# First weights' split moved ahead of the turned tiles in the opening of a hybrid encoder step

## Chip, cores and metric

One core of one Trainium2 chip runs the whole step in one launch. The metric is the device time in microseconds of that launch; the figures below are the median of three runs of the kernel before, its spread, and one profiled execution.

## The reference, cut to what matters

One layer of a streaming encoder is computed for a prompt of 512 frames and for 64 frames of a running stream, D = 1024. The opening is the first two lines of this:

```python
xn = rmsnorm(x, attn_pre_norm)     # x * rsqrt(mean(x*x) + eps) * gain
h = xn @ w_in                      # 1024 columns to keys, values, queries, gates, ...
# gated linear attention, indexed sparse attention, merge
x = x + rmsnorm(mixed, attn_post_norm)
f, conv_new = conv_ffn(rmsnorm(x, ffn_pre_norm), conv_prev, w_up, conv_w, conv_b, w_down)
x = x + rmsnorm(f, ffn_post_norm)
```

## The kernel before, in words

The program is written engine by engine, each engine's instructions in a fixed order, tied together by semaphores that each stand in the code. SP issues most transfers, ScalarE (ACT), VectorE (DVE) and GpSimd (POOL) compute, TensorE (PE) multiplies.

The 576 tokens stand in five tiles: tile 0 holds the 64 sample tokens, tiles 1 to 4 the prompt. TensorE multiplies rounded values (fp32r). To keep fp32 accuracy each operand is held as a rounded part and a remainder: `whi` and `wlo` for weights, `xhi` and `xlo` (both in the tile `xs`) for the turned samples. A product is then three matmuls. The weights come in panels through two buffers of `raw`; a panel's split is a copy with rounding on ACT (`split(p)`, line 960) and a subtraction on DVE (line 1531).

In the opening each tile tt takes these steps. SP loads it (`load_x`, line 607). ACT squares and sums it (`square`, line 975) and takes the root (`root`, line 980). DVE takes the reciprocal and scales the tile by it and by the gain, in two halves (`head`, lines 1542 and 1547); the gain row was spread over all partitions by PE into banks 3 and 4 (line 2124). PE turns the tile with eight transposes, two halves of four (`turn`, line 2111). ACT copies each half out with rounding (`turned`, line 987), and DVE takes the remainder (`rest`, line 1557).

The turned halves go through three PSUM banks in rotation: half t = 2 * tt + kh is in bank 5 + t % 3. So half 3, the second half of tile 1, uses the bank of half 0, and PE waits ahead of it for DVE's remainder of half 0:

```python
pe.wait_ge(xn_ready, t + 1)
if t >= 3:
    pe.wait_ge(xlo_ready, t - 2)
```

PE's order is: gain row, turn(0), turn(1), two products of the identity with itself into a bank that is overwritten afterwards (line 2145), eight products of the first weights' rounded part with tiles 0 and 1 (line 2134), the remainder products of tile 0 (lines 2139 and 2141), turn(2), those of tile 1, turn(3), then the other tiles with the first panel (lines 2087 to 2089), turn(4) among them, and the second panel. The first panel ("kv", 0) comes in four pieces, SP's first four `raw` transfers (line 620).

SP issues in this order: the gain row, tiles 0 and 1, the first panel, tiles 2 to 4, the second panel, the caches. Then it waits until all ten halves have their remainder (`xlo_ready` at 10) before it goes on with the small weight at line 663 and with panel after panel, each of which waits for the split two panels back.

Behind the opening come the other input panels with index scores, attention and the linear recurrence between them, the merge, and the ConvFFN with its products of w_up and w_down.

Of the kernel before, what the change touches and what calls it, by code (L numbers as in the profile page):

```python
# [18 lines left out]
P = 128  # L19
# [32 lines left out]
def tok(tt):  # L52

    return slice(0, P) if tt == 0 else slice(DEC + P * (tt - 1), DEC + P * tt)
# [7 lines left out]
def rows(tt):  # L62
    return DEC if tt == 0 else P
# [212 lines left out]
def splits(p):  # L276

    return p + 1 if p < DOWN0 else p + 1 - SEVENS
# [22 lines left out]
def layer_kernel(nc, A, O):  # L301
# [6 lines left out]
    with ExitStack() as ctx:  # L308
        base = (nc.sbuf_base + 63) // 64 * 64

        def at(name, shape, dtype, offset):
            size = 4
            for d in shape[1:]:
                size *= d
            assert base + offset + size <= nc.sbuf_usable_end, name
            return nc.alloc_sbuf_tensor_at(name, shape, dtype, offset=base + offset)

        def sem(name):
            return ctx.enter_context(nc.semaphore(name))

        ps = ctx.enter_context(nc.psum_tensor("ps", [P, 8, 512], F32))
# [9 lines left out]
        ident = at("ident", [P, P], F32, o)  # L331
# [48 lines left out]
        gain_row = at("gain_row", [P, D], F32, o3 + 5888)  # L380
# [50 lines left out]
        gpre_loaded, coefs_loaded, cache_loaded = sem("gpre_loaded"), sem("coefs_loaded"), sem("cache_loaded")  # L431
# [98 lines left out]
        def panel_size(p):  # L530
            kind, i = PANELS[p]
            return {"kv": 1360, "wb": 1024, "down": 512 * i[2] if kind == "down" else 0}.get(kind, 2048)

        def loaded(p):

            return 16 * sum(len(panel_loads(q)) for q in range(p % 2, p + 1, 2))
# [31 lines left out]
        def wait_panel_used(eng, p):  # L568

            kind, i = PANELS[p]  # L570
            if kind == "kv":
                eng.wait_ge(*((panel_used, 1) if i == 0 else (kv_done, TILES)))
            elif p < BRANCH0:
                eng.wait_ge(unit_done, 1 + max(s.unit for s in SLOTS if s.panel == p))
            elif p < OUT0:
                eng.wait_ge(unit_done, UNITS1 + 2 * (p - BRANCH0) + 2)
            elif UP0 <= p < DOWN0 and seven(p - UP0):
                eng.wait_ge(prod_done[3], p - UP0 - SEVEN0 + 1)
            elif UP0 <= p < DOWN0:
                eng.wait_ge(unit_done, UNITS2 + plain_rows_done((p - UP0) // 2, (p - UP0) % 2, 1))  # L580
            else:
                name, value = job_signal([j for j in JOBS if j.panel == p][-1])
                eng.wait_ge({"wide_done": wide_done, "panel_used": panel_used}[name], value)
# [20 lines left out]
        def _(sp):  # L604
            def load_x(tt):
                src = A["x_sample"][0] if tt == 0 else A["x_prompt"][0, P * (tt - 1):P * tt, :]
                sp.dma_start(x_tok[0:rows(tt), tt, :], src).then_inc(x_loaded[tt], 16)
# [32 lines left out]
                sp.wait_ge(saved_summed, 4 * k + 4)  # L640
                sp.dma_start(sums_dram[k], saved[b][:, :]).then_inc(saved_out[b % 2], 16)

            sp.dma_start(gain_row[0:1, :], A["attn_pre_norm"]).then_inc(gpre_loaded, 16)
            load_x(0)
            load_x(1)
            for p in range(UP0 + SEVEN0):
# [297 lines left out]
        def _(act):  # L944
# [7 lines left out]
            def split(p):  # L952

                if p >= NP:
                    return
                act.wait_ge(raw_loaded[p % 2], loaded(p))
                if p >= 2:
                    wait_panel_used(act, p - 2)
                n = panel_size(p)
                nc.scalar.activation(whi[:, p % 2, 0:n], raw[:, p % 2, 0:n], ACT.Copy).then_inc(hi_ready, 1)  # L960
# [4 lines left out]
            def preload_sqrt():  # L965

                nc.scalar.activation(table_probe, eps, ACT.Sqrt).then_inc(tables_in, 1)


            act.wait_ge(stats_primed, 2)  # L970
            preload_sqrt()

            def square(tt):
                act.wait_ge(x_loaded[tt], 16)
                nc.scalar.activation(junk[0:rows(tt), :], x_tok[0:rows(tt), tt, :], ACT.Square,
                                     accum_out=ssq[0:rows(tt), tt:tt + 1]).then_inc(sumsq_ready, 1)
                act.wait_ge(sumsq_ready, tt + 1)

            def root(tt):
                nc.scalar.activation(rstd[:, tt:tt + 1], ssq[:, tt:tt + 1], ACT.Sqrt, scale=1.0 / D, bias=eps).then_inc(root_ready, 1)  # L980

            def turned(tt):
                for kh in range(2):
                    t = 2 * tt + kh
                    act.wait_ge(x_turned, t + 1)
                    n = rows(tt)
                    nc.scalar.activation(xhi[:, 4 * kh:4 * kh + 4, tok(tt).start:tok(tt).start + n],
                                         ps[:, 5 + t % 3, :].rearrange("p (k c) -> p k c", k=4)[:, :, 0:n], ACT.Copy).then_inc(xhi_ready, 1)
# [2 lines left out]
            root(0)  # L991
            square(1)
            root(1)
            turned(0)
            split(0)
            turned(1)
            for tt in range(2, TILES):
                square(tt)
# [516 lines left out]
        def _(dve):  # L1515
            chain = [0]

            def link(ins):
                chain[0] += 1
                ins.then_inc(dve_chain, 1)  # L1520
                dve.wait_ge(dve_chain, chain[0])

            def split(p):

                if p >= NP:
                    return
                dve.wait_ge(hi_ready, splits(p))
                if p - 1 in POOL_SPLITS:
                    dve.wait_ge(lo_ready, p)
                n = panel_size(p)  # L1530
                nc.vector.tensor_tensor(wlo[:, p % 2, 0:n], raw[:, p % 2, 0:n], whi[:, p % 2, 0:n].bitcast(F32),  # L1531
                                        ALU.subtract).then_inc(lo_ready, 1)
# [4 lines left out]
            def head(tt):  # L1537

                k = rows(tt)
                c = slice(tt, tt + 1)  # L1540
                dve.wait_ge(root_ready, tt + 1)
                link(nc.vector.reciprocal(rstd[:, c], rstd[:, c]))
                for kh in range(2):
                    if tt == 0:
                        dve.wait_ge(gain_spread, kh + 1)
                    f = slice(512 * kh, 512 * kh + 512)
                    nc.vector.scalar_tensor_tensor(out=x_tok[0:k, tt, f], in0=x_tok[0:k, tt, f], scalar=rstd[0:k, c],
                                                   in1=ps[0:k, 3 + kh, :], op0=ALU.mult, op1=ALU.mult).then_inc(xn_ready, 1)

            def rest(tt):  # L1550

                for kh in range(2):
                    t = 2 * tt + kh
                    k = rows(tt)
                    dve.wait_ge(xhi_ready, t + 1)
                    c = slice(tok(tt).start, tok(tt).start + k)
                    nc.vector.tensor_tensor(xlo[:, 4 * kh:4 * kh + 4, c], ps[:, 5 + t % 3, :].rearrange("p (k c) -> p k c", k=4)[:, :, 0:k],  # L1557
                                            xhi[:, 4 * kh:4 * kh + 4, c].bitcast(F32), ALU.subtract).then_inc(xlo_ready, 1)
# [3 lines left out]
            nc.vector.memset(ssq, 1.0).then_inc(stats_primed, 1)  # L1562
            head(0)
            head(1)
            rest(0)
            split(0)
            rest(1)
            for tt in range(2, TILES):
                head(tt)
# [497 lines left out]
        def _(pe):  # L2067
# [73 lines left out]
                    ins = pe.matmul(ps[:, tt, 0:340], xhi[:, k, tok(tt)], first_lo[:, k, :], start=False, stop=False)  # L2141
                return ins

            for _ in range(2):
                pe.matmul(ps[:, 2, 0:P], ident[:, :], ident[:, :], start=True, stop=True)
            pe.wait_ge(hi_ready, 1)
            pe.wait_ge(xhi_ready, 3)
            rounded_products(0)
# [403 lines left out]
```

## Time and profile before

| | us |
|---|---|
| median of 3 runs | 973.52 |
| lowest to highest | 973.52 to 974.26 |
| profiled execution, its own time | 974.0 |
| span of the profiled execution, first to last instruction | 972.3 |

The span runs from the first to the last instruction of the program; all starts below count from its beginning. PE is TensorE's matmuls, PEld its weight loads, which run beside them. Engines with a q (SPq) are the sequencers that issue transfers. A timeline row is: start, duration, engine, line, operation, output <- inputs, shapes, count, and in brackets the idle time of the engine ahead of it and what ended it. One row can hold several instructions in a row of the same kind; its duration then is that of all of them.

### The profile page before, as it was taken

Reading aid. Unit: us, or ns where it says so; the run is one execution under the profiler, and the core shown is the slowest. Engines: PE = TensorE matmul, PEld = TensorE weight load, DVE = VectorE, ACT = ScalarE, POOL = GpSimd, SP = SyncE. Lnnn points to the kernel's source line nnn. Section 1 sums busy time; section 2 is a strip of 40 time slices with the busy share of each in tenths; the row PEclk is TensorE's granted clock in tenths of the full one; section 3 lists DMA queues with packets and bytes.
Section 4 is the critical chain, followed back from the end, with each engine's and each line's share of the span. In section 5 each row is a group of like instructions: output and inputs, shape, how many; then the busy total and the mean of one; then the engine's idle time right before and its main releaser. Section 6 shows DMA issues by size and latency. Waiting matters only on the chain.

```text
span 972.3 us, 17124 instructions
## 1 busy us (share of the span) xinstructions
PE 955.3 (98%) x6550; PEld 904.3 (93%) x6550; DVE 617.5 (64%) x997; ACT 476.3 (49%) x800; POOL 181.0 (19%) x301
## 2 busy tenths in 40 slices
PE   8999999999999999999999999999999999999997
PEld 6999998889999999999998899999999999788886
DVE  6278878745344368924455679688888889723214
ACT  6356436777322256421124558566666667522112
POOL 3104423323122111101001146211111112100000
PEclk9999999999999999999999999999999999999999
DMA  6812121112376458766446352244443344412323
GB/s 169 205 45 87 44 88 44 44 44 67 122 235 223 139 209 268 262 242 227 125 135 239 129 174 87 76 121 127 150 123 119 119 128 131 145 36 84 137 70 119
DMA packets 121980, 129.75 MB, mean 133 GB/s; under 512 B 14884, under 2 KB 103828, under 8 KB 119619
## 3 DMA queue, kind: packets, MB, share of 16 engines
q1 hardware_dynamic: 115474, 105.97, 35.0%
q0 software_dynamic: 6448, 22.99, 6.7%
q8 instruction: 39, 0.64, 0.3%
q14 instruction: 19, 0.15, 0.0%
HBM read 105.84 MB, written 23.11 MB: 133 GB/s over the span
## 4 chain that ended last, share of the span: by engine, by line
PE 90%; DVE 4%; ACT 3%; issue 2%; DMA 0%; POOL 0%; DVEq 0%; SPq 0%; ACTq 0%; POOLq 0%
PE ps L2078 11%; PE ps L2080 11%; PE ps L2079 11%; PE ps L2443 7%; PE ps L2445 7%; PE ps L2444 7%; PE ps L2087 7%; PE ps L2089 7%; PE ps L2088 7%; PE ps L2283 2%; PE ps L2097 1%; PE ps L2098 1%; PE ps L2420 1%; PE ps L2419 1%; PE ps L2418 1%
## 5 line engine op out<-in xcount | busy, mean ns | idle before, releaser
L2078 PE MATMUL ps<-xs,whi 128*128 128x288 f32 x608 | 183.4, 302 | 0.0
L2080 PE MATMUL ps<-xs,wlo 128*128 128x288 f32 x608 | 179.1, 295 | 0.0
L2079 PE MATMUL ps<-xs,whi 128*128 128x288 f32 x608 | 179.0, 294 | 0.0
L1531 DVE TENSOR_TENSOR wlo<-raw,whi 128x2048 fp32r<-128x2048 f32 (+2 forms) x36 | 78.9, 2193 | 107.9 <-ACT whi L960 107.9
L960 ACT ACTIVATE whi<-raw 128x2048 fp32r<-128x2048 f32 (+2 forms) x47 | 86.1, 1833 | 99.3 <-PE ps L2089 76.4
L2078 PEld LDWEIGHTS ps<-xs,whi 128*128 128x128 f32 x608 | 114.2, 188 | 0.7
L2079 PEld LDWEIGHTS ps<-xs,whi 128*128 128x128 f32 x608 | 114.2, 188 | 0.4
L2080 PEld LDWEIGHTS ps<-xs,wlo 128*128 128x128 f32 x608 | 114.0, 188 | 0.0
L2087 PE MATMUL ps<-whi,xs 128*128 128x256 f32 (+2 forms) x224 | 72.7, 325 | 0.1
L2089 PE MATMUL ps<-wlo,xs 128*128 128x256 f32 (+2 forms) x224 | 71.2, 318 | 0.0
L2088 PE MATMUL ps<-whi,xs 128*128 128x256 f32 (+2 forms) x224 | 71.2, 318 | 0.0
L789 POOL TENSOR_TENSOR wlo<-raw,whi 128x512 fp32r<-128x512 f32 x36 | 45.8, 1303 | 128.6 <-ACT whi L960 128.6
L2089 PE MATMUL ps<-wlo,us 128*128 128x512 f32 x176 | 69.5, 395 | 0.0
L2087 PE MATMUL ps<-whi,us 128*128 128x512 f32 x176 | 69.5, 395 | 0.0
L2088 PE MATMUL ps<-whi,us 128*128 128x512 f32 x176 | 69.5, 395 | 0.0
L2445 PE MATMUL ps<-ts,wlo 128*128 128x288 f32 x216 | 63.9, 296 | 0.0
L2444 PE MATMUL ps<-ts,whi 128*128 128x288 f32 x216 | 63.7, 295 | 0.0
L2443 PE MATMUL ps<-ts,whi 128*128 128x288 f32 x216 | 63.5, 294 | 0.0
L2087 PEld LDWEIGHTS ps<-whi,xs 128*128 128x128 f32 x224 | 42.5, 190 | 3.2 <-DVE xs L1557 0.4
L2089 PEld LDWEIGHTS ps<-wlo,xs 128*128 128x128 f32 x224 | 42.5, 190 | 2.5
L2088 PEld LDWEIGHTS ps<-whi,xs 128*128 128x128 f32 x224 | 42.5, 190 | 2.4
L1040 ACT ACTIVATE stage<-ps 128x576 f32<-128x576 f32 x24 | 15.6, 652 | 57.6 <-PE ps L2080 57.6
(370 smaller groups left out, 2616.8 us busy)
## 6 DMA issues: line engine op xcount, KB each, us to landing
raw<-in_w_in SPq DMA_DIRECT2D x21, 1024.0 KB, 5.8
raw<-in_w_down SPq DMA_DIRECT2D x10, 1024.0 KB, 5.0
saved<-in_w_up SPq DMA_DIRECT2D x36, 256.0 KB, 4.3
sums_scratch<-saved SPq DMA_DIRECT2D x9, 1024.0 KB, 4.8
raw<-sums_scratch SPq DMA_DIRECT2D x9, 1024.0 KB, 4.8
qraw<-in_w_up SPq DMA_DIRECT2D x27, 256.0 KB, 2.9
raw<-in_w_up SPq DMA_DIRECT2D x13, 512.0 KB, 4.0
raw<-in_w_up SPq DMA_DIRECT2D x26, 256.0 KB, 4.5
```

The costliest lines, as they stand in the source:

```text
L789: ins = nc.gpsimd.tensor_tensor(wlo[:, p % 2, c], raw[:, p % 2, c], whi[:, p % 2, c].bitcast(F32), ALU.subtract)
L960: nc.scalar.activation(whi[:, p % 2, 0:n], raw[:, p % 2, 0:n], ACT.Copy).then_inc(hi_ready, 1)
L1531: nc.vector.tensor_tensor(wlo[:, p % 2, 0:n], raw[:, p % 2, 0:n], whi[:, p % 2, 0:n].bitcast(F32), ALU.subtract).then_inc(lo_ready, 1)
L2078: pe.matmul(out, wh[:, k, c0:c0 + P], xh[:, k, t], start=(k == 0), stop=False)
L2079: pe.matmul(out, wh[:, k, c0:c0 + P], xl[:, k, t], start=False, stop=False)
L2080: ins = pe.matmul(out, wl[:, k, c0:c0 + P], xh[:, k, t], start=False, stop=(k == kn - 1))
L2087: pe.matmul(out, xh[:, k0 + k, t], wh[:, k, :], start=(first and k == 0), stop=False)
L2088: pe.matmul(out, xl[:, k0 + k, tl or t], wh[:, k, :], start=False, stop=False)
L2089: ins = pe.matmul(out, xh[:, k0 + k, t], wl[:, k, :], start=False, stop=(last and k == kn - 1))
L2443: pe.matmul(out, wh[:, c], xh[:, k, :], start=(opens and k == 0), stop=False, skip_group_check=True)
L2444: pe.matmul(out, wh[:, c], xl[:, k, :], start=False, stop=False, skip_group_check=True)
L2445: ins = pe.matmul(out, wl[:, c], xh[:, k, :], start=False, stop=(k == 3), skip_group_check=True)
```

## The change

The gain row's transfer goes from the head of SP's queue to the head of ACT's, ahead of ACT's table load. On SP the two first tiles therefore stand first. On ACT and on DVE the split of the first panel moves from behind the first tile's copy or remainder to ahead of it. The two products of the identity on PE are taken out.

```diff
@@ sync
-            sp.dma_start(gain_row[0:1, :], A["attn_pre_norm"]).then_inc(gpre_loaded, 16)
             load_x(0)
             load_x(1)
@@ scalar
+            act.dma_start(gain_row[0:1, :], A["attn_pre_norm"]).then_inc(gpre_loaded, 16)
             act.wait_ge(stats_primed, 2)
             preload_sqrt()
...
             root(0)
             square(1)
             root(1)
+            split(0)
             turned(0)
-            split(0)
             turned(1)
@@ vector
             head(0)
             head(1)
+            split(0)
             rest(0)
-            split(0)
             rest(1)
@@ tensor
-            for _ in range(2):
-                pe.matmul(ps[:, 2, 0:P], ident[:, :], ident[:, :], start=True, stop=True)
             pe.wait_ge(hi_ready, 1)
             pe.wait_ge(xhi_ready, 3)
             rounded_products(0)
```

## Rows read from the trace of the kernel before

**Rows 1.** The page, busy time: us, share of the span, instructions.
```profile
PE 955.3 (98%) x6550; PEld 904.3 (93%) x6550; DVE 617.5 (64%) x997; ACT 476.3 (49%) x800; POOL 181.0 (19%) x301
```

**Rows 2.** Busy time by stretch: length; PE, PEld, DVE, ACT, POOL; clock, DMA share, GB/s.
```profile
23.30:972.30 949.00, 936.09 (x6454) 888.83 (x6454) 601.75 (x968) 460.35 (x771) 173.18 (x280) 1.00 0.42 132
```

**Rows 3.** Waits of SP's queue up to 40 us: us in total, times, longest.
```profile
SPq L663 <- DVE xs L1557: 9.2, 1, 9.2
```

**Rows 4.** The chain that ended last, up to 60 us: start, us, what.
```profile
12.00 2.15 PE ps L2134 x8
14.15 0.62 PE ps L2139 x4
...
23.30 0.42 PE ps L2087
```

**Rows 5.** Timeline of ACT, 4.5 to 18.5 us.
```profile
4.96 1.06 ACT L975 ACTIVATE junk<-x_tok 64x1024 f32<-64x1024 f32 x1 [2.66 <-DMA x_tok<-in_x_sample]
...
7.51 0.29 ACT L980 ACTIVATE small<-small 128x1 f32<-128x1 f32 x1
...
9.36 1.34 ACT L960 ACTIVATE whi<-raw 128x1360 fp32r<-128x1360 f32 x1
...
11.68 1.05 ACT L975 ACTIVATE junk<-x_tok 128x1024 f32<-128x1024 f32 x1
...
12.85 0.30 ACT L980 ACTIVATE small<-small 128x1 f32<-128x1 f32 x1
...
14.22 0.29 ACT L980 ACTIVATE small<-small 128x1 f32<-128x1 f32 x1
15.87 1.09 ACT L987 ACTIVATE xs<-ps 128x512 fp32r<-128x512 f32 x2 [1.36 <-PE ps L2111]
16.85 1.06 ACT L975 ACTIVATE junk<-x_tok 128x1024 f32<-128x1024 f32 x1
```

**Rows 6.** Timeline of SP's queue, 0 to 4 us.
```profile
0.81 0.35 SPq L643 DMA_DIRECT2D gain_row<-in_attn_pre_norm  x1
1.22 0.57 SPq L607 DMA_DIRECT2D x_tok<-in_x_sample  x1
...
2.46 1.53 SPq L620 DMA_DIRECT2D raw<-in_w_in  x3
```

**Rows 7.** Line 620, 4.05 to 4.5 us: the first panel's last piece; ns, starts.
```profile
L620 SPq DMA_DIRECT2D raw<-in_w_in x1: 507/507/507, 4.0 to 4.0; - x1
...
DMA to landing us min/median/max: 5.3/5.3/5.3
```

**Rows 8.** Timeline of PE's weight loads, 9 to 11 us.
```profile
8.98 0.71 PEld L2111 LDWEIGHTS ps<-ident,x_tok 128*128 128x128 f32 x4 [0.35 <-DVE x_tok L1547]
10.03 0.71 PEld L2111 LDWEIGHTS ps<-ident,x_tok 128*128 128x128 f32 x4 [0.34 <-issue]
```

**Rows 9.** Timeline of DVE, 9.4 to 9.8 us.
```profile
9.50 0.42 DVE L1557 TENSOR_TENSOR xs<-ps,xs 128x256 fp32r<-128x256 f32 x1
```

**Rows 10.** Busy time by stretch, as rows 2, around the change of pace.
```profile
12.00:13.80 1.80, 1.80 (x9) 1.80 (x8) 1.76 (x5) 1.77 (x4) 0.00 (x0) 1.00 1.13 309
14.10:15.20 1.10, 1.10 (x9) 1.10 (x8) 1.06 (x4) 0.38 (x2) 0.00 (x0) 1.00 1.22 235
```

**Rows 11.** Timeline of PE's matmuls, 2 to 16 us.
```profile
2.40 3.75 PE L2124 MATMUL ps<-gain_row,ones_row 1*128 1x512 f32 x4 [2.40 <-DMA gain_row<-in_attn_pre_norm]
...
8.98 2.17 PE L2111 MATMUL ps<-ident,x_tok 128*128 128x128 f32 x8 [0.17 <-DVE x_tok L1547]
10.94 1.06 PE L2145 MATMUL ps<-ident 128*128 128x128 f32 x4
...
15.24 1.03 PE L2111 MATMUL ps<-ident,x_tok 128*128 128x128 f32 x8
```

**Rows 12.** Timeline of DVE, 6 to 18 us.
```profile
8.18 1.41 DVE L1547 SCALAR_TENSOR_TENSOR x_tok<-x_tok,small,ps 128x512 f32<-128x512 f32 x2
...
10.73 1.58 DVE L1531 TENSOR_TENSOR wlo<-raw,whi 128x1360 fp32r<-128x1360 f32 x1 [0.48 <-ACT whi L960]
...
13.61 1.41 DVE L1547 SCALAR_TENSOR_TENSOR x_tok<-x_tok,small,ps 128x512 f32<-128x512 f32 x2
```

## The prediction

> **What bounds the kernel now.** The page first: TensorE (PE) is busy 98% of the span [rows 1]. Then the busy time from 23.3 us on: 936.1 of 949.0 us [rows 2]. From there PE runs almost without a gap, and what feeds it is released by work of the opening: SP's next panel loads wait until DVE has made the last remainder of the turned samples [rows 3]. So what the opening loses or wins at 23.3 us is carried to the end nearly one to one; I see nothing behind it that starts at a fixed time. All of the change lies ahead of 23.3 us.
>
> There I read the chain of waits [rows 4] beside ACT's timeline [rows 5]: x_sample lands, ScalarE (ACT) squares it, later PE multiplies and turns tile 2; ACT copies that out at 15.87 and squares tile 4 at 16.85, and through DVE the chain reaches PE's dense stream at 23.30. The number to keep is square(4) at 16.85: from it to 23.30 stands a fixed string of ACT and DVE work.
>
> Five more readings decide this case. SP issues the weight row at 0.81 and x_sample at 1.22 [rows 6]. The last piece of the first weights is issued at 4.0 and lands 5.3 us later [rows 7], and ACT's split(0) starts at 9.36 [rows 5], as soon as they are there; I put the landing at 9.34. PE's weight loads for the second half of turn(1) stood idle 0.34 us until 10.03 [rows 8]: by the code that half fills bank 5, which rest(0)'s first half on DVE has to read first (line 2108, xlo_ready at least 1), and that instruction ended at 9.92 [rows 9]. Last, the pace: eight rounded products take 2.15 us on the chain, 0.27 each, the next four 0.62, 0.155 each [rows 4]. For 340 columns those are TensorE's two levels, 1.2 and 2.4 GHz, though the granted clock reads 1.00 in both stretches [rows 10]. The rise is at 13.9.
>
> **Weight row and samples.** SP loses one issue of 0.35 us; its other transfers start 0.41 us earlier (1.22 to 0.81). They are issued one behind another without a pause [rows 6], so I move their landings by as much: first weights at 8.93. On ACT one issue is added ahead of the table load; ACT stands idle 2.66 us before x_sample lands [rows 5], which hides it. PE's weight-row products run 3.75 us from 2.40, to 6.15 [rows 11]; the second half of DVE's first normalising needs them at about 6.9, so a row up to 0.8 us later costs nothing.
>
> Here a rule speaks against the change. The rows show the 4 KB alone at the head of one queue, landed by 2.40 [rows 6, 11]. The Trainium skill (DMA: Bandwidth & Descriptors, Queues, rings and completion order) says that each DMA engine takes the queues that have work in turn, a packet of each, so that a row in ACT's queue shares with x_sample. Were it so slow that it landed only with x_sample, at 4.55, its products would end at 8.3, the second tile's normalising near 10.6, and DVE would be about 0.2 us late for its split: the sum below would be larger by 0.2. I take zero, because the row is 4 KB against 256 KB.
>
> **The moved splits, step by step.** ACT ends root(1) at 7.80 [rows 5], then at 7.4. Now split(0) stands next, and its weights land at 8.93: ACT waits 1.5 us, runs 1.34, ends at 10.29. Only then come turned(0)'s two copies and the first copy of turned(1).
> DVE ends head(1) near 9.2 (8.18 + 1.41 - 0.41 [rows 12]); its split(0) waits for ACT until 10.32 and runs 1.58, to 11.90. Only then does rest(0) read bank 5: its first half takes 0.42 and starts 0.09 ahead of the end of the work before it (9.50 against head(1)'s 9.59 [rows 9, 12]), so it ends at 12.23 instead of 9.92.
> So PE's second half of turn(1) goes from 10.03 to about 12.35, and PE, which ran through this stretch, stands idle from 9.7 to there. ACT's second copy of turned(1) and square(2) behind it move as far: square(2) from 11.68 to 14.0. Queued behind that are both roots and square(3): root(3), which ended at 14.51, now ends at 16.8 [rows 5]. Turned(2) began at 15.87 after an idle 1.36 us; that cover is used up.
>
> **The dummies.** The two ident products (1.06 us from 10.94 [rows 11]) go. They save nothing, since PE now stands idle where they stood.
>
> **Products and pace.** The rounded products start 0.91 us behind turn(1)'s second half, as the dummies did (10.03 to 10.94): 13.25, against 12.0. Between there and turn(2) stand 8 rounded and 8 remainder products. turn(2) starts 1.61 us ahead of square(4) (15.24 to 16.85 [rows 5, 11]).
> Low end: the pace rises at 13.9 as before. Two or three products run slow, the others fast, done at 16.05; but turn(2)'s second half needs head(2), which follows square(2): root(2) ends 1.47 behind square(2)'s start [rows 5], so at 15.47; normalised by 17.1 (0.2 more, then 1.41 [rows 12]). That gives square(4) at 18.25: 1.4 us later.
> High end: slow all the way. Sixteen products of 0.28 end at 17.8, turn(2)'s transposes run as slowly as turn(1)'s (2.17 for eight [rows 11]), and square(4) comes at 20.1: 3.3 us later.
> I take a rise as far behind the restart as it lay before: from turn(1)'s first transpose at 8.98 to 13.9; from 12.35 that gives 17.3. Fourteen products are slow, turn(2) starts at 17.56, square(4) at 19.17: 2.3 us later. I am nearer to that end because before, too, transposes and products stood densely and stayed slow for that long. Counted from turn(1)'s second half alone (10.03), the rise falls at 16.2 and the loss is 1.8.
>
> **Sum.** The 0.4 us of the earlier loads is already inside; the net is +2.3 us. The profiled execution took 974.0 us (972.3 of span and 1.7 around it), 0.5 above the median of 973.52. I set the 2.3 on the middle of these two, 973.76: 976.0 us. A measurement here tells 0.2% from no change, 1.95 us on either side of 973.52: 971.57 to 975.47.
>
> **Rivals.**
> A, not slower: the same wait, but PE's pace has risen between 13.9 and 16.2. The place is the sixteen products ahead of turn(2); the price falls to 1.4 to 1.8 us, and it decides if fewer than about eleven of them run at the slow pace. On 973.52 that is 974.9 to 975.3, inside 0.2%. For it: the rise stood at 13.9 before, and nothing shows that it hangs on turn(1). Against it: 2.7 us of new idle time stand right ahead of it.
> B, the weights land much earlier, by the time ACT reaches its split at 7.4 (1.5 us better than I have it). Then DVE's split runs from 9.2 and rest(0)'s first half ends at 11.1; the loss falls to about 1.0: 974.5. Against it: the weights are queued behind 768 KB of samples, so that issuing them 0.41 us earlier brings 0.41.
> C, slower still: the pace stays low past turn(2), 3.3 us, 977.1. Against it: PE's work has no pause from 12.35 on.
> D, a gain: the 0.41 us of earlier loads reach the end whole, because turn(1)'s second half does not stand behind DVE's split. The code says that it does (line 2108). It would give 973.1, and no edit here is worth the 1.95 us that a measurable gain needs.
>
> **How the numbers follow.** Forecast (2 to 2.8 us): 0.5. C: 0.18. A: 0.22. B: 0.07. D and anything faster: 0.03. Forecast and C make it slower by over 0.2%: 0.68. A and B make no difference: 0.29. The last 0.03 I give to faster, though D itself stays within 0.2%. The range runs from 974.7 (A's 974.9 less the 0.2 us by which the landing may be off) to 977.3 (C's 977.1 and the same 0.2).
>
> **What would show it.** In the changed trace: x_sample issued at 0.81; ACT's split(0) at 8.9 with some 1.5 us of idle time before it that ends with raw's landing; DVE's split(0) ahead of the first remainder in xs; PE idle from 9.7 to about 12.35; square(2) at 14.0 and square(4) near 19.2; the dense stream from 25.6 instead of 23.3. How many of the sixteen products stand 0.28 us apart and how many 0.155 tells forecast, A and C apart. I am wrong if PE's second half of turn(1) starts before 11.5, if the loss at square(4) is not found again at the dense stream's start, or if it is made up behind it.

## The result, and the profile after

The changed kernel is slower: 975.34 us, median of 18 runs (974.85 to 977.81), against 973.85 for the kernel before, measured beside it (18 runs, 973.00 to 974.77). The ratio is 1.0019, with an interval of 1.0011 to 1.0026. The forecast was 976.0, within 974.7 to 977.3: the direction and the mechanism hold, the size came out at 1.5 us instead of 2.3 and just under the 0.2% that I had called measurable.

The profiled execution took 975.11 us (span 973.4). The chain that ended last, up to 60 us; columns are start, us, what. It answers to [rows 4].

```profile
3.65 5.28 DMA raw<-in_w_in
8.95 1.34 ACT whi L959
10.31 1.57 DVE wlo L1531
11.89 0.35 DVE xs L1557
12.37 1.09 PE ps L2111 x4
13.46 2.27 PE ps L2134 x8
15.72 0.73 PE ps L2139 x4
16.45 0.62 PE ps L2141 x4
...
24.98 0.42 PE ps L2087
```

Before, this chain began with the samples, as this line of it shows:

```profile
1.22 3.72 DMA x_tok<-in_x_sample
```

Now it begins with the first weights, goes through both splits and the remainder of half 0 (DVE's xs at 11.89) and only then to PE's second half of turn(1). The dense stream starts at 24.98 instead of 23.30 [rows 4]: 1.68 us later.

ACT's timeline, 4 to 19 us, against [rows 5]:

```profile
4.41 1.06 ACT L975 ACTIVATE junk<-x_tok 64x1024 f32<-64x1024 f32 x1 [1.55 <-DMA x_tok<-in_x_sample]
...
8.95 1.34 ACT L959 ACTIVATE whi<-raw 128x1360 fp32r<-128x1360 f32 x1 [1.69 <-DMA raw<-in_w_in]
10.19 1.13 ACT L987 ACTIVATE xs<-ps 128x256 fp32r<-128x256 f32 x3
13.49 0.60 ACT L987 ACTIVATE xs<-ps 128x512 fp32r<-128x512 f32 x1 [2.18 <-PE ps L2111]
13.99 1.05 ACT L975 ACTIVATE junk<-x_tok 128x1024 f32<-128x1024 f32 x1
...
17.55 1.09 ACT L987 ACTIVATE xs<-ps 128x512 fp32r<-128x512 f32 x2 [0.72 <-PE ps L2111]
18.52 1.06 ACT L975 ACTIVATE junk<-x_tok 128x1024 f32<-128x1024 f32 x1
```

Read the brackets: ACT waits 1.69 us for the weights, for which it did not have to wait before, then 2.18 us for PE's turn. square(2) (13.99) is 2.3 us later than in [rows 5], square(4) (18.52) 1.67.

DVE's timeline, 6 to 16 us, against [rows 9, 12]:

```profile
10.31 1.57 DVE L1531 TENSOR_TENSOR wlo<-raw,whi 128x1360 fp32r<-128x1360 f32 x1 [1.28 <-ACT whi L959]
11.81 1.35 DVE L1557 TENSOR_TENSOR xs<-ps,xs 128x256 fp32r<-128x256 f32 x3
```

PE's timeline, 2 to 18 us, against [rows 11]:

```profile
2.33 3.75 PE L2124 MATMUL ps<-gain_row,ones_row 1*128 1x512 f32 x4 [2.33 <-DMA gain_row<-in_attn_pre_norm]
...
8.43 1.11 PE L2111 MATMUL ps<-ident,x_tok 128*128 128x128 f32 x4 [0.17 <-DVE x_tok L1547]
12.37 1.09 PE L2111 MATMUL ps<-ident,x_tok 128*128 128x128 f32 x4 [2.83 <-DVE xs L1557]
13.11 2.62 PE L2134 MATMUL ps<-whi,xs 128*128 128x340 f32 x8
15.52 0.93 PE L2139 MATMUL ps<-whi,xs 128*128 128x340 f32 x4
16.29 0.78 PE L2141 MATMUL ps<-wlo,xs 128*128 128x340 f32 x4
16.91 1.03 PE L2111 MATMUL ps<-ident,x_tok 128*128 128x128 f32 x8
```

turn(1), one row of eight before, is now two rows of four with 2.83 us of idle time between, ended by DVE's xs. That is where the loss arises; it is not its size, since by square(4) 1.67 us of it are left. The eight rounded products stand 0.28 us apart (2.27 on the chain), the four behind them take 0.73 and the last four 0.62: nine of the sixteen ran at the low pace.

SP's queue: the samples start first, at the time of the weight row before [rows 6], and the next load stands at 25.55 instead of 23.87, because it waits for the last remainder as in [rows 3] (second fence: SP's waits up to 40 us).

```profile
0.82 0.59 SPq L607 DMA_DIRECT2D x_tok<-in_x_sample  x1
```

```profile
SPq L662 <- DVE xs L1557: 11.2, 1, 11.2
```

Behind the opening the 1.6 us stay: ACT's instructions are 1.65 later at 800 us. From there to the end the difference between the two profiled executions shrinks to 1.1. All eleven other kernels of the experiments, whatever their edit, gain the same 0.55 to 0.57 us there on that one execution of the kernel before, so it belongs to that execution and is nothing that the change gives back.

**Runs in two groups.** The 18 runs are not one heap. Each run lists its mean granted clock; 14 have 0.999 and lie between 974.85 and 975.71, four have 0.997 and lie between 976.95 and 977.81. The kernel before has such runs too (27 of the 106 that stood beside the experiments). So the experiments are read by group, since a median over all runs mixes the two. They ran in four sessions; the last column is the kernel before beside them, at 0.998 or more, and the differences below are taken from it. These groups were formed after the runs were seen, and reading by group leaves out what an edit does to the share of runs in the lower one: 8 of 12 in fill_gap beside 7 of 35 of the kernel before, 6 of 10 in own_bank beside 8 of 33. Whether an edit causes that is not shown.

| kernel | runs at 0.998 or more: number, median | at 0.997 or less: number, median | ratio of all, interval | before beside it, 0.998 or more |
|---|---|---|---|---|
| before, all four sessions | 79, 973.64 | 27, 974.51 | | |
| changed | 14, 975.25 | 4, 977.67 | 1.0019, 1.0011 to 1.0026 | clocks not listed |
| gain_only | 7, 973.09 | 4, 974.02 | 0.9997, 0.9988 to 1.0006 | 973.60 |
| order_only | 9, 976.08 | 1, 978.79 | 1.0027, 1.0017 to 1.0036 | 973.60 |
| no_dummies | 7, 973.16 | 5, 975.86 | 1.0008, 0.9998 to 1.0017 | 973.60 |
| own_bank | 4, 973.47 | 6, 976.25 | 1.0016, 1.0006 to 1.0026 | 973.60 |
| fill_gap | 4, 974.33 | 8, 976.80 | 1.0019, 1.0011 to 1.0028 | 973.82 |
| own_bank_busy | 6, 973.51 | 6, 975.11 | 1.0006, 0.9998 to 1.0015 | 973.82 |
| dve_first | 7, 975.08 | 4, 977.76 | 1.0023, 1.0014 to 1.0032 | 973.82 |
| gain_warm | 8, 973.28 | 3, 974.52 | 0.9998, 0.9989 to 1.0007 | 973.82 |
| act_first | 6, 974.00 | 5, 976.50 | 1.0014, 1.0005 to 1.0023 | 973.49 |
| gain_bank_busy | 8, 973.01 | 3, 974.27 | 0.9997, 0.9988 to 1.0006 | 973.49 |
| gain_nodm | 9, 972.69 | 3, 975.65 | 0.9993, 0.9985 to 1.0002 | 973.75 |

### The profile page after: what moved, and what is told of

Same layout as the page of the kernel before. It is cut to its first block, busy times and chain, and to the rows that moved or that the text cites. A ratio compares the mean times of both kernels' runs of the same rounds, so it can differ in the third digit from the quotient of the medians.

```text
span 973.4 us, 17116 instructions
## 1 busy us (share of the span) xinstructions
PE 954.1 (98%) x6546; PEld 904.2 (93%) x6546; DVE 617.8 (63%) x997; ACT 475.9 (49%) x800; POOL 181.0 (19%) x301
## 4 chain that ended last, share of the span: by engine, by line
PE 89%; DVE 4%; ACT 3%; issue 2%; DMA 1%; SPq 0%; POOL 0%; DVEq 0%; ACTq 0%; POOLq 0%
PE ps L2078 11%; PE ps L2080 11%; PE ps L2079 11%; PE ps L2441 7%; PE ps L2443 7%; PE ps L2442 7%; PE ps L2087 7%; PE ps L2088 6%; PE ps L2089 6%; PE ps L2281 2%; PE ps L2098 1%; PE ps L2097 1%; PE ps L2418 1%; PE ps L2416 1%; PE ps L2417 1%
```

## The experiments

### The change taken apart: gain_only, order_only, no_dummies

gain_only is the kernel before with this alone:

```diff
-            sp.dma_start(gain_row[0:1, :], A["attn_pre_norm"]).then_inc(gpre_loaded, 16)
...
+            act.dma_start(gain_row[0:1, :], A["attn_pre_norm"]).then_inc(gpre_loaded, 16)
             act.wait_ge(stats_primed, 2)
```

> Only the weight row goes to ScalarE's queue; splits and dummies stay as before. Theory 1 (the bank: DVE's split ahead of rest(0) holds bank 5, which the second half of turn(1) needs) and theory 2 (the pace: without the dummies PE's faster pace comes later): neither is touched, so the loads come 0.41 us earlier and all else with them: first weights at 8.9, square(4) on ACT at 16.4 instead of 16.85, dense stream from 22.9, about 973.4 against 973.85. Theory 3 (the queue: the row in ACT's queue lands late behind x_sample): the weight-row products start after 2.9, normalising and square(4) come later than before, 974.0 or more.

Its square(4) and its dense stream (22.94) both start 0.36 earlier than before:

```profile
16.49 1.06 ACT L975 ACTIVATE junk<-x_tok 128x1024 f32<-128x1024 f32 x1
```

Runs at the higher clock: 973.09, 0.5 below the kernel before. Theory 3 falls: PE's weight-row products start at 2.31, so the row comes in time from ACT's queue. Over all runs the gain can't be told from nothing.

order_only is the kernel before with both splits moved:

```diff
-            turned(0)
             split(0)
+            turned(0)
             turned(1)
...
-            rest(0)
             split(0)
+            rest(0)
             rest(1)
```

> Only the splits are moved on ACT and DVE; the weight row stays on SP and the two dummies stay. Theory 1: the weights land at 9.34, rest(0)'s first half ends at 12.64, PE's second half of turn(1) starts at 12.8, square(2) at 14.4, square(4) at about 19.4 (2.5 later than before), about 976.3. Theory 2: the dummies are there, so no loss: square(4) at 17.0 or less, 973.9. Theory 3: the row is on SP, so no loss either.

PE's matmuls of that kernel, 8 to 19 us, and its square(4):

```profile
8.97 1.12 PE L2111 MATMUL ps<-ident,x_tok 128*128 128x128 f32 x4 [0.17 <-DVE x_tok L1547]
13.01 1.08 PE L2111 MATMUL ps<-ident,x_tok 128*128 128x128 f32 x4 [2.92 <-DVE xs L1557]
13.89 1.06 PE L2145 MATMUL ps<-ident 128*128 128x128 f32 x4
...
17.01 1.14 PE L2139 MATMUL ps<-whi,xs 128*128 128x340 f32 x4
```

```profile
20.22 1.06 ACT L975 ACTIVATE junk<-x_tok 128x1024 f32<-128x1024 f32 x1
```

The same hole of 2.9 us, with the dummies in place and the row on SP. The time rises to 976.08, 2.5 above the kernel before, as expected. The traced execution (976.80) lost more: square(4) is 3.4 later than before where 19.4 (2.5 later) was expected; in it the pace rose only at 17.8. The order alone makes the loss; the other two parts of the change made it smaller.

no_dummies is the kernel before without the two identity products:

```diff
-            for _ in range(2):
-                pe.matmul(ps[:, 2, 0:P], ident[:, :], ident[:, :], start=True, stop=True)
```

> Only the two identity products are taken out. Theory 1: the rounded products start at 11.2 instead of 12.0; turn(2) can gain at most 0.2 us, since its second half waits for head(2) until 15.0; the pace may rise anywhere from 13.9 to 15; square(4) between 16.6 and 17.2, 973.6 to 974.3. Theory 2: the pace rises about 2 us later than 13.9, as it did in the changed kernel (15.85), square(4) at 17.8 or later, about 975.

In its profile the pace rises at 13.7, and square(4) starts 0.3 earlier than before:

```profile
16.56 1.06 ACT L975 ACTIVATE junk<-x_tok 128x1024 f32<-128x1024 f32 x1
```

At the higher clock: 973.16, 0.4 below the kernel before. So taking them out does not cost 1.5 us in those runs, and theory 2 falls as the cause of the loss. But the five runs at the lower clock have a median of 975.86, 2.7 above the others, where the kernel before loses 0.9: over all runs nothing is won.

Added up at the higher clock: -0.51 (row) +2.48 (order) -0.44 (products) = +1.53. The changed kernel has +1.49 by the medians of all its runs and the runs beside it, and +1.6 by its higher group against the 973.64 of all sessions.

### The wait itself: own_bank

The changed kernel with a bank of its own for the second half of tile 1, so that PE has nothing to wait for:

```diff
+        def turn_bank(t):
+
+            return 2 if t == 3 else 5 + t % 3
...
-                    if t >= 3:
+                    if t >= 4:
                         pe.wait_ge(xlo_ready, t - 2)
...
-                        ins = pe.transpose(ps[:, 5 + t % 3, P * j:P * j + k], x_tok[0:k, tt, P * f:P * f + P], ident[0:k, 0:k])
+                        ins = pe.transpose(ps[:, turn_bank(t), P * j:P * j + k], x_tok[0:k, tt, P * f:P * f + P], ident[0:k, 0:k])
```

> The changed kernel with a bank of its own (bank 2) for the second half of tile 1, so that PE need not wait for rest(0) there. Theory 1: that half is turned at about 9.6 instead of 12.4, square(2) starts at 11.8 instead of 14.0, square(4) between 16.6 and 17.5 instead of 18.5, about 974.1, 1.2 us below the changed kernel. Theories 2 and 3: nothing changes, 975.3.

PE's matmuls, 8 to 18 us, and from the chain the start of the dense stream:

```profile
8.57 1.97 PE L2115 MATMUL ps<-ident,x_tok 128*128 128x128 f32 x8 [0.17 <-DVE x_tok L1551]
11.39 2.60 PE L2138 MATMUL ps<-whi,xs 128*128 128x340 f32 x8 [0.85 <-ACT xs L991]
```

```profile
23.30 0.42 PE ps L2091
```

turn(1) is one row of eight again, and the dense stream starts at 23.30, to the hundredth where it stood before, though both splits are still ahead and the dummies gone. At the higher clock 973.47, 0.1 below the kernel before beside it and 1.8 below the changed kernel. Together with the trace that shows the bank as the place of the loss in those runs. Over all runs nothing is won: the median of the ten is 975.68, not below the changed kernel's 975.34, because six of them fell into the lower group, at 976.25. The expectation of 974.1 holds for neither group as it stands: the higher one lies 0.6 below it, the lower one 2.2 above.

### Which engine's order: dve_first, act_first

The changed kernel with ACT's order as before (dve_first), or with DVE's order as before (act_first):

```diff
-            split(0)
             turned(0)
+            split(0)
             turned(1)
```

> The changed kernel with ScalarE's order as before (turned(0), split(0), turned(1)) and only DVE's split ahead of rest(0). The bank theory puts the loss on DVE's split alone: the second half of turn(1) still starts at 12.4, square(2) at 14.0, square(4) at 18.5, 975.3 as the changed kernel. If ScalarE's order is what costs, that half starts at 9.5 and the time falls to 973.5.

```diff
-            split(0)
             rest(0)
+            split(0)
             rest(1)
```

> The changed kernel with DVE's order as before (rest(0), split(0), rest(1)) and only ScalarE's split ahead of turned(0). By the bank theory rest(0) now waits for ScalarE's copies behind the split and not for DVE's own split: its first half ends at 11.0, the second half of turn(1) starts at 11.1 (9.4 to 10.0 before, 12.4 changed), square(2) at 12.75, square(4) at 16.9 to 17.6, the dense stream at 23.4 to 24.1: about half of the loss, 974.0 to 974.6. If ScalarE's order alone makes the loss, that half starts at 12.4 and the time is 975.3; if DVE's alone makes it, the half starts before 10 and the time is 973.5.

PE's matmuls of dve_first and then of act_first, 8 to 18 and 8 to 19 us:

```profile
12.36 1.08 PE L2111 MATMUL ps<-ident,x_tok 128*128 128x128 f32 x4 [2.83 <-DVE xs L1557]
```

```profile
11.27 1.09 PE L2111 MATMUL ps<-ident,x_tok 128*128 128x128 f32 x4 [1.50 <-DVE xs L1557]
12.01 2.62 PE L2134 MATMUL ps<-whi,xs 128*128 128x340 f32 x8
14.43 1.33 PE L2139 MATMUL ps<-whi,xs 128*128 128x340 f32 x4
15.56 1.33 PE L2141 MATMUL ps<-wlo,xs 128*128 128x340 f32 x4
```

DVE's split alone makes the whole hole (12.36, 2.83 us); dve_first stands at 975.08, the changed kernel at 975.25. With ACT's split alone the hole is 1.50 us and the time 974.00, 0.5 above the kernel before. Of the two moves DVE's is the one to take back first; with DVE's in place, these runs show no clear difference from ACT's order. The profiled execution of act_first is one of the lower group: there all sixteen products ran at the low pace (2.62, 1.33 and 1.33), and square(4) came at 18.35 instead of the 16.9 to 17.6 expected.

### The pace: fill_gap, own_bank_busy, gain_warm

fill_gap is the changed kernel with PE kept at work through the wait:

```diff
+                    if t == 3:
+                        for _ in range(6):
+                            pe.matmul(ps[:, 2, 0:P], ident[:, :], ident[:, :], start=True, stop=True)
                     if t >= 3:
                         pe.wait_ge(xlo_ready, t - 2)
```

> The changed kernel with six products of the identity (into bank 2, which is overwritten later) between the two halves of turn(1), so that PE works through the wait for the bank. The bank's wait stays. If the late rise of the pace comes from PE's idle stretch: the pace rises by 14 in every run, products no longer hold turn(2), which then waits for head(2); square(4) at 18.2 to 18.3 (18.5 in the changed kernel's profile, 16.85 before), times between 974.6 and 975.6 and none above 976.5, where the changed kernel had 4 of 18 at 976.95 to 977.81. If the idle stretch has nothing to do with it: the same spread with a group near 977.5.

PE's matmuls, 8 to 18 us, and square(4):

```profile
9.32 2.77 PE L2109 MATMUL ps<-ident 128*128 128x128 f32 x12
12.08 1.12 PE L2114 MATMUL ps<-ident,x_tok 128*128 128x128 f32 x4
12.84 1.89 PE L2137 MATMUL ps<-whi,xs 128*128 128x340 f32 x8
14.58 0.78 PE L2142 MATMUL ps<-whi,xs 128*128 128x340 f32 x4
15.20 0.79 PE L2144 MATMUL ps<-wlo,xs 128*128 128x340 f32 x4
16.23 1.31 PE L2114 MATMUL ps<-ident,x_tok 128*128 128x128 f32 x8 [0.24 <-DVE x_tok L1547]
```

```profile
18.08 1.05 ACT L975 ACTIVATE junk<-x_tok 128x1024 f32<-128x1024 f32 x1
```

The pace rises at 13.7, six of the sixteen products earlier than in the changed kernel, and then turn(2) waits for DVE's x_tok: this is the low end of my sum. square(4) starts 1.2 later than before (1.4 forecast for that end), and at the higher clock the time is 974.33, 0.5 above the kernel before. The rest of the expectation failed: eight of twelve runs lie between 975.9 and 977.4. So the second group is there without the hole, and more often than in the changed kernel.

own_bank_busy is own_bank with the two products put back, into bank 1:

```diff
+            for _ in range(2):
+                pe.matmul(ps[:, 1, 0:P], ident[:, :], ident[:, :], start=True, stop=True)
             pe.wait_ge(hi_ready, 1)
```

> The changed kernel with a bank of its own for the second half of tile 1, and with the two identity products put back (into bank 1). Two-part theory (the bank's wait costs 1.7 us, PE's idle stretch lets the pace rise late in some runs): both parts are gone, all runs between 972.8 and 974.6, none above 975.5; with the bank alone 6 of 10 were at 975.6 to 977.1. If the second group has another cause than PE's idle time: about half of the runs stay above 975.5.

The second group is still there, six of twelve, but at 975.11, 1.1 lower than without the products. The expectation that it would go has failed. Its profile is one of that group, and yet the pace rose there earlier than in any other, at 11.8 (PE's matmuls, 8 to 18 us):

```profile
11.54 1.64 PE L2138 MATMUL ps<-whi,xs 128*128 128x340 f32 x8
```

gain_warm is gain_only with two more identity products ahead of turn(0):

```diff
+            for _ in range(2):
+                pe.matmul(ps[:, 2, 0:P], ident[:, :], ident[:, :], start=True, stop=True)
             turn(0)
```

> The kernel before with the weight row on ScalarE's queue and two more identity products between the weight-row products and turn(0), so that PE has less idle time from 2.3 on. If the pace rises earlier by it (before 10): turn(1) takes about half as long, the sixteen products are through by 14.0, turn(2) waits for head(2) until 14.4, square(4) at 16.0 instead of 16.5, about 973.1, 0.5 below the weight row alone (973.65). If those products do not bring the rise forward: square(4) at 16.5 or up to 0.3 later where they stand ahead of turn(0), 973.6 to 974.

They run from 6.05 to 7.27, and the pace rises at 13.7 all the same; square(4) at 16.49 is that of gain_only. In this profile, work that early brought no earlier rise.

### Versions to beat both: gain_bank_busy, gain_nodm

gain_bank_busy is gain_only with own_bank's bank and the two products into bank 1; its diffs stand above.

> A candidate to beat both: the order of the kernel before, the weight row on ScalarE's queue, bank 2 for the second half of tile 1 and the two identity products kept, into bank 1. Loads 0.41 us earlier and no wait of 0.1 to 0.3 us for the bank: square(4) at 16.2 to 16.5, the dense stream at 22.7 to 22.95, 973.2 over all runs, 0.4 to 0.6 below the kernel before and not told from it for sure. If the bank mattered in the order of before as well, the dense stream would start before 22.5.

973.01 at the higher clock, 0.5 below the kernel before, as gain_only is below its own; its dense stream started at 23.17, later than expected, in a profile whose weights landed only at 9.81. So the bank is worth something only where a split stands ahead of rest(0).

gain_nodm is the changed kernel with both splits back in their places.

> The changed kernel with both splits back in their places: only the weight row moved and the two identity products gone. If the parts add up (in runs with a mean clock of 0.998 or 0.999: weight row -0.5, products gone -0.4, order +2.5), those runs have a median near 972.7, 2.5 below the changed kernel (975.25) and 0.9 below the kernel before (973.60). If the products keep PE's pace, the runs at 0.996 or 0.997 stand 2 to 3 us above the others, near 975.5, as without the products alone, and not 1 us as in the kernel before, so that the median of all runs is not told from the kernel before. If the order cost nothing by itself, all runs are at 975.3.

PE's matmuls, 8 to 19 us, and the dense stream from the chain:

```profile
8.49 2.17 PE L2111 MATMUL ps<-ident,x_tok 128*128 128x128 f32 x8 [0.17 <-DVE x_tok L1547]
11.07 2.37 PE L2134 MATMUL ps<-whi,xs 128*128 128x340 f32 x8 [0.42 <-ACT xs L987]
```

```profile
22.61 0.42 PE ps L2087
```

972.69 at the higher clock, 972.73 over all twelve runs beside 974.00 for the seventeen of the kernel before that ran with it; the ratio is 0.9993 with an interval of 0.9985 to 1.0002. It is the lowest of all and 2.6 us below the changed kernel. At the higher clock its nine runs (972.15 to 973.18) all lie below the nine of the kernel before (973.35 to 974.00), but over all runs its gain is not clear of noise.

Its three other runs have a median of 975.65, 3.0 above the nine. That was expected for a kernel without the two identity products, and the table bears it out: the lower group stands 0.9 to 1.6 us above the higher one in the five kernels with these products right ahead of the rounded products (before, gain_only, gain_warm, gain_bank_busy, own_bank_busy), and 2.4 to 3.0 in the seven without (changed, no_dummies, own_bank, fill_gap, dve_first, act_first, gain_nodm). order_only has the products and 2.7, from a single run. How the products do that is not shown.

## Why the prediction was right, and where it missed

**Loads.** x_sample was issued at 0.82 and the weights landed at 8.93 (8.93 forecast). The weight row on ACT cost nothing: PE's products with it started at 2.33, and at 2.30 to 2.58 in all ten traces with the row on ACT's queue, beside 2.33 to 2.51 in the three with it on SP's. The Trainium skill (DMA: Bandwidth & Descriptors, Queues, rings and completion order) says that each DMA engine serves the queues that have work in turn, a packet of each. The trace shows no delay from it here, so the 0.2 us by that rule are not in the result.

**The chain through bank 5.** Every step came where the prediction put it: ACT's wait 1.69 us (1.5), DVE's split at 10.31 (10.32), PE's second half of turn(1) at 12.37 (12.35), square(2) at 13.99 (14.0). own_bank takes the wait away, and in the runs at the higher clock the loss with it; dve_first and act_first put it on DVE's split.

**The dummies.** I wrote that taking them out saves nothing. In the changed order that fits: with PE idle for 2.8 us there is no place where they cost. By themselves they cost 0.4 to 0.55 us at the higher clock, in no_dummies and again between gain_only and gain_nodm (0.51 and 1.06 below the kernel before). At the lower clock it is the other way round: no_dummies stands at 975.86, where the kernel before beside it has 974.68, so over all runs taking them out won nothing.

**The mis-sized term: the pace.** "I take a rise as far behind the restart as it lay before: from turn(1)'s first transpose at 8.98 to 13.9; from 12.35 that gives 17.3." In the traced execution it rose at 15.8, 3.5 us behind the restart. Nine products were slow instead of fourteen, turn(2) started at 16.91 instead of 17.56, and the term measured 1.67 us at square(4) in place of 2.3. That is rival A's case (fewer than eleven slow products, 1.4 to 1.8 us), to which I had given 0.22.

The step failed because there is no such fixed distance. Behind a restart the rise came after 3.4 us in dve_first, 3.5 in the changed kernel, 4.8 in order_only and 5.5 in act_first; behind turn(1)'s first transpose, where there is no hole, after 3.2 (own_bank_busy) to 5.6 (own_bank). The 4.9 that I took lay inside that spread, so a single execution could have met it, and order_only's lost 3.4. What sets the moment stays open. The low end of the term holds: with the rise at 13.7, fill_gap lost 1.2 where I had 1.4. The high end was summed too low. With turn(2)'s second half 1.1 behind its first and square(4) 1.65 behind that, as square(2) is in [rows 5, 8], 17.8 gives 20.5 and not 20.1, so C should have been 3.7 us and the range's upper end 977.7. That the measured time fell inside the range is owed to its having both ends of this term in it, not to the distance chosen between them.

**The carry to the end.** 1.67 at square(4), 1.68 at the dense stream, 1.65 at 800 us, 1.5 to 1.6 in the medians: nothing behind the opening took it back. From square(4) to the dense stream it is 6.45 us before, 6.46 in the changed kernel, 6.45 in order_only and 6.44 in fill_gap, the fixed string that the prediction named.

**The verdict between slower and no change.** I gave slower by over 0.2% the most, and the ratio of 1.0019 lies just below, with 1.002 inside its interval. It was the size of one term, not the sign, that decided this.

## What to carry to other kernels

When a step is moved ahead on an in-order engine, look not only at who waits for that step but at who waits for what it now stands in front of: here a split of 1.6 us got in front of an instruction of 0.4 us that released a bank. Ahead of a load, ask when it lands; an engine that had its weights just in time has nothing to gain from asking for them earlier. And look at each run's granted clock before a difference of one or two microseconds is believed, and then also at how many runs each kernel has at either clock.

## What the runs showed of the hardware

The group at the lower mean clock has an event of its own, in the attention stage. Busy time by stretch for fill_gap (mean clock 0.996), then for the changed kernel (0.999) and for the kernel before (0.999); columns as in [rows 2]:

```profile
200.00:204.00 4.00, 1.78 (x15) 1.58 (x14) 0.53 (x1) 3.97 (x8) 2.69 (x4) 1.00 0.29 62
204.00:208.00 4.00, 3.94 (x21) 3.93 (x22) 3.86 (x8) 1.25 (x3) 0.00 (x0) 0.61 0.58 203
```

```profile
200.00:204.00 4.00, 2.18 (x19) 1.98 (x17) 0.10 (x1) 3.96 (x8) 3.11 (x4) 1.00 0.16 33
204.00:208.00 4.00, 3.51 (x29) 3.51 (x30) 3.90 (x7) 1.32 (x3) 0.00 (x0) 1.00 0.68 230
```

```profile
200.00:204.00 4.00, 1.69 (x14) 1.48 (x13) 1.68 (x3) 3.37 (x7) 1.47 (x3) 1.00 0.60 176
```

PE is about half idle from 200 to 204 in all three. Behind that the granted clock stood at 0.61 from 204 to 208 in fill_gap and at 1.00 in the changed kernel. ACT's copies behind it stand 2.77 us later than in the kernel before, those ahead of it 1.22: the fall cost 1.6 us. The profiles of own_bank_busy and act_first show the same place and the same price (1.6 each), and the ten with 0.999 show no fall there. How busy PE was in that stretch does not tell the two apart: the kernel before kept its clock at 1.69, own_bank_busy lost it at the same 1.69. What does is not shown. fill_gap's clock fell a second time, at 167 us, and that cost nothing: ACT's instructions were 1.22 later than in the kernel before at 150 us and again at 195.

Why the two groups lie 0.9 us apart in the kernel before and 2.4 in the changed one stays open, beyond what gain_nodm shows of the two identity products. A rise in the opening that comes late together with the fall at 204 is not the rule: of the three profiles with the fall, act_first has the rise at 16.8, fill_gap at 13.7 and own_bank_busy at 11.8, the earliest of all. No execution of the kernel before at the lower clock was profiled.

In the opening the clock's row read 1.00 [rows 10] while products of 340 columns stood 0.28 us apart, before and after. That 1.00 is not a reading. The trace's own record of the granted clock, from which the row is made, begins only with the rise: its first entry, full clock, stands at 13.87 us in the kernel before and at 15.84 in the changed one, and at the change of pace in all thirteen traces. Ahead of that entry the level has to be read from the distance of like instructions.
